# Unread products out where their operand was there already, modulation factors spread at waits, output projections by tile, LayerNorm statistics by halves

## The reference

```python
def first_block(x, p, positions, w_in, w_o, ...):
    for i in range(DEPTH):
        h = x @ w_in[i]
        q, k, v, qi, ki, wi, u, vs = jnp.split(h, split_points, axis=-1)
        ...
        a_out = dsa_attention(q, k, v, qi, ki, wi)
        b_out = spatial_gating(jax.nn.gelu(u), jax.nn.gelu(vs), sgu_w[i], sgu_b[i], ...)
        mix = jnp.concatenate([a_out, b_out], axis=-1) @ w_o[i]
        x = layer_norm(ALPHA * x + mix, ln1_g[i], ln1_b[i])
        gate, up = jnp.split(x @ w_ffn_in[i], 2, axis=-1)
        ffn = (jax.nn.silu(gate) * up) @ w_ffn_out[i]
        ple = (p[i] @ w_ple[i]) * jax.nn.sigmoid(x @ w_ple_gate[i])
        x = layer_norm(ALPHA * x + ffn + ple, ln2_g[i], ln2_b[i])

def second_block(x, c, positions, ada_w, ada_b, ...):
    for layer in range(DEPTH):
        mod = cond @ ada_w[layer] + ada_b[layer]
        sh1, sc1, g1, sh2, sc2, g2 = jnp.split(mod, 6, axis=-1)
        h = modulate(rms_norm(x, norm_mix[layer]), sh1, sc1)
        y = even_mixer(h, ...) if layer % 2 == 0 else odd_mixer(h, ...)
        x = x + g1[:, None, :] * y
        h = modulate(rms_norm(x, norm_mlp[layer]), sh2, sc2)
        x = x + g2[:, None, :] * squared_relu_mlp(h, mlp_w1[layer], mlp_w2[layer])
```

## Time and profile before

| | |
|---|---|
| three runs | 1359.42, 1356.29, 1351.66 us; median 1356.29 |
| profiled execution | 1356.18 us; span 1354.4 us, mean granted clock 0.994 |
| PE, PEld | 1308.6 us (97%), 1072.3 us (79%) |
| DVE, ACT, POOL | 921.8 us (68%), 655.2 us (48%), 113.7 us (8%) |
| unread products (L1507) | 191, 51.8 us busy |

### The profile page before, as it was taken

One profiled execution on the slowest core, in us unless ns is written; L12 is line 12 of the kernel. 1 busy time (PEld: TensorE's weight loads), 2 busy tenths in 40 slices (PEclk: granted clock), 3 DMA queues, 4 the chain that ended last, 5 costly groups with the idle time before them and its releaser, 6 DMA issues.

```text
span 1354.4 us, 16107 instructions
## 1 busy us (share of the span) xinstructions
PE 1308.6 (97%) x6466; PEld 1072.3 (79%) x6466; DVE 921.8 (68%) x1237; ACT 655.2 (48%) x886; POOL 113.7 (8%) x146
## 2 busy tenths in 40 slices
PE   8999999998999999999998989999999998999998
PEld 6877888887877788888798867888887766888886
DVE  5967777766685777775779756866666985644444
ACT  6644444443563544444475444544446554654542
POOL 2001000000000100000234200000004500000000
PEclk9999999999999999999999999999999999999999
DMA  9615677873642578885263303876764421445450
GB/s 373 235 63 195 241 307 308 309 275 129 224 142 98 214 265 308 308 308 209 84 210 117 109 32 114 323 295 244 299 248 170 160 105 34 173 174 184 182 186 31
DMA packets 41114, 270.36 MB, mean 200 GB/s; under 512 B 4656, under 2 KB 4672, under 8 KB 12880
## 3 DMA queue, kind: packets, MB, share of 16 engines
q1 hardware_dynamic: 38288, 259.83, 52.1%
q0 software_dynamic: 2464, 8.98, 1.9%
q10 hardware_dynamic: 288, 0.52, 0.1%
HBM read 268.27 MB, written 1.05 MB: 199 GB/s over the span
## 4 chain that ended last, share of the span: by engine, by line
PE 84%; DVE 10%; ACT 3%; issue 2%; POOL 1%; DMA 0%; ACTq 0%; DVEq 0%; POOLq 0%
PE ps L1540 49%; PE ps L1530 25%; PE ps L1554 4%; DVE WB L1852 3%; PE ps L1639 2%; PE ps L1507 2%; PE ps L1615 1%; ACT E L1652 1%; DVE st L2062 1%; DVE st L2134 1%; ACT WB L1652 1%; ACT XTH L1652 1%; DMA GB<-xTd 0%; POOL st L1455 0%; DVE X L2151 0%
## 5 line engine op out<-in xcount | busy, mean ns | idle before, releaser
L1852 DVE TENSOR_TENSOR WB<-RAW,WB 128x2048 fp32r<-128x2048 f32 (+3 forms) x211 | 453.4, 2151 | 247.3 <-ACT WB L1652 246.9
L1652 ACT ACTIVATE WB<-RAW 128x2048 fp32r<-128x2048 f32 (+3 forms) x211 | 379.7, 1802 | 200.4 <-PE ps L1540 198.7
L1530 PE MATMUL ps<-WB,XTH 128*128 128x512 f32 (+3 forms) x1176 | 314.5, 389 | 11.0 <-ACT XTH L1652 8.7
L1540 PE MATMUL ps<-WB,XTH 128*128 128x512 f32 (+3 forms) x1176 | 305.3, 381 | 7.1 <-DVE WB L1852 7.0
L1540 PE MATMUL ps<-WB,XTL 128*128 128x512 f32 (+3 forms) x1176 | 303.7, 379 | 0.0
L1540 PEld LDWEIGHTS ps<-WB,XTH 128*128 128x128 f32 x1176 | 218.4, 189 | 48.1 <-DVE WB L1852 9.8
L1530 PEld LDWEIGHTS ps<-WB,XTH 128*128 128x128 f32 x1176 | 213.6, 190 | 49.7 <-ACT XTH L1652 11.4
L1540 PEld LDWEIGHTS ps<-WB,XTL 128*128 128x128 f32 x1176 | 218.9, 189 | 38.4
L1530 PE MATMUL ps<-WB,HTH 128*128 128x512 f32 (+1 forms) x452 | 127.0, 396 | 0.5 <-ACT HTH L1652 0.5
L1540 PE MATMUL ps<-WB,HTH 128*128 128x512 f32 (+1 forms) x452 | 126.5, 395 | 0.0
L1540 PE MATMUL ps<-WB,HTL 128*128 128x512 f32 (+1 forms) x452 | 126.4, 394 | 0.0
(11 more groups left out here) (177 smaller groups left out, 973.9 us busy)
## 6 DMA issues: line engine op xcount, KB each, us to landing
RAW<-W SPq DMA_DIRECT2D x220, 1024.0 KB, 4.9
RAW<-W SPq DMA_DIRECT2D x22, 768.0 KB, 4.3
VEC<-vecd POOLq DMA_DIRECT2D x10, 512.0 KB, 7.5
RAW<-W SPq DMA_DIRECT2D x8, 512.0 KB, 3.5
RAW<-W SPq DMA_DIRECT2D x4, 576.0 KB, 3.8
RAW<-W SPq DMA_DIRECT2D x2, 648.0 KB, 3.8
T<-sgwd POOLq DMA_DIRECT2D x2, 512.0 KB, 8.1
X<-xd SPq DMA_DIRECT2D x1, 1024.0 KB, 17.7
```

What stands on the lines that cost most here:

```text
L1530: eng.matmul(banks[b][:, 0:cw], x2[j][0], hi[:, j, c0:c0 + cw], start=first and j == 0, stop=False)
L1540: op = eng.matmul(banks[b][:, 0:cw], x2[j][0 if low_w else 1], (lo if low_w else hi)[:, j, c0:c0 + cw], start=False, stop=last and end and ...
L1652: return eng.activation(dst, src, f, **k)
L1852: eng.tensor_tensor(WB[:, it["raw"], 0:w], RAW[:, it["raw"], 0:w], WB[:, it["high"], 0:w].bitcast(F32), ALU.subtract).then_inc(*up("wl", n))
```

## The change

- Unread products: 191 before, 76 now. They are left out in front of turns of E, of projections and of transposes at 38 places and made fewer at four; the 11 at each of the three projections that open a stage of the second block become 2.
- Modulation factors: the transposes of `gain` leave the two input projections of the second block, where they were woven in as eight groups of four. Each factor is now made in one piece of eight transposes: one in the dilated attention, between the scores of its first two units, one ahead of each of the two MLPs' first projections and one ahead of the odd layer's input projection, the last three in the places of the unread products.
- `linear_k` goes by tile for w_o and the even output projection: all its items for tile 0, then all for tile 1; before, both tiles of an item came one after the other. The bank of a tile is taken when the tile starts.
- LayerNorm: the statistics of a half are taken right behind the addition that completes it. In the first block's layer 0, the low part of the next weights is issued ahead of the second LayerNorm's passes over tile 1.
- `hold`: in the odd layer's second attention the low parts are issued from the third step on.

```diff
-        def linear_k(name, lhs, evac, ready, turned=False):
+
+        def linear_k(name, lhs, evac, ready, turned=False, by_tile=True):
             its = chunk_items(name)
             assert len(its) <= cur["pairs"]
-            w, g, ps = its[0]["w"], uid(), [take(), take()]
+            w, g, ps = its[0]["w"], uid(), [None, None]
             advance()
             its = its[::-1] if turned else its
-            for it in its:
-                for t in range(2):
-                    yield from ready(it["a"], t)
-                    b, fr = ps[t]
-                    lows([it])
-                    do("mm", it, t, "x", [(b, 0, w, (g, t) if it is its[-1] else None)], it is its[0], it is its[-1],
-                       wanted(lhs[t], "x", it), fr if it is its[0] else [], 0, it is its[-1], t)
-                    if t:
-                        used(it)
-                        advance(1)
-                    if it is its[-1]:
-                        evac(t, b, ("mm", (g, t)))
-                    yield
+            for it, t in ([(it, t) for t in range(2) for it in its] if by_tile else
+                          [(it, t) for it in its for t in range(2)]):
+                yield from ready(it["a"], t)
+                if ps[t] is None:
+                    ps[t] = take()
+                b, fr = ps[t]
...
-        def attention(units, scale, filler=None, steps=1, pads=(), first=0, between=()):
+        def attention(units, scale, filler=None, steps=1, pads=(), first=0, between=(), hold=0):
...
-                    turns(units[k - 1], pads[k - 1] if k <= len(pads) else 2)
+                    turns(units[k - 1], pads[k - 1] if k <= len(pads) else 0)
...
-                if k < n - 2:
+                if hold <= k < n - 2:
                     lows(old)
...
+        ln_sts = [None, None]
+
+
+        def ln_half(key, t, c, after):
+            if c == 0:
+                ln_sts[t] = col(12)
+            do("ln_half", key, t, c, ln_sts[t], after)
+
+        def ln_tile(key, t, between=None, before=None, halfway=None):
+            mv = col(2)
+            do("ln_stats", key, ln_sts[t], mv)
...
-                fill = linear2("w_in", "x", xt_w, [put_sel, put_gelu(1)], mid_in, pad=(6, 0), mid_at=2)
+                fill = linear2("w_in", "x", xt_w, [put_sel, put_gelu(1)], mid_in, pad=(2, 0), mid_at=2)
...
-                              [("kd", (i, t, 2))] + t_pe, 6, t, pad=0 if t else 2)
+                              [("kd", (i, t, 2))] + t_pe, 6, t, pad=i if t == 0 else 0)
...
-                             [("kd", (i, t, 1))] + t_pe, 0, t, pad=0 if t else 2)
+                             [("kd", (i, t, 1))] + t_pe, 0, t)
...
+                    ln_half((i, 1, t), t, c, rw[t][-1])
                     if c and t:
-                        x_n[1] = ln_tile((i, 1, 1), 1, rw[1], halfway=lambda: advance(1))
+                        x_n[1] = ln_tile((i, 1, 1), 1, halfway=lambda: advance(1))
...
-            attention(units, 0.125, fill, first=3)
+            attention(units, 0.125, fill, first=1, pads=(0, 2, 2))
...
-            run(linear2("w_ple_gate", "x", xt_w, [put_g(0), put_g(1)], mid1, pad=(0, 3), mid_at=1))
+            run(linear2("w_ple_gate", "x", xt_w, [put_g(0), put_g(1)], mid1, mid_at=1))
...
+                ln_half((i, 2, t), t, c, ("add_out", (i, t, c)))
                 if c == 0:
                     return
 
                 def between():
                     if t and i == 0:
                         xt_w[0][:] = to_XT(X, 8, x_n[0], 0)
+                        advance(1)
 
                 before = norm_sums(0, x_n[0]) if t and i else None
-                x_n[t] = ln_tile((i, 2, t), t, [("add_out", (i, t, c)) for c in range(2)], between, before,
-                                 (lambda: go(0, pad=14)) if t and i else None)
-                if t:
+                x_n[t] = ln_tile((i, 2, t), t, between, before, (lambda: go(0, pad=14)) if t and i else None)
+                if t and i:
...
+        def gain(layer, k):
             assert len(mod_w[(layer, 3 * k + 2)]) == 4
-            if hf == 0:
-                vg_w[k] = []
-            g = uid()
-            b, fr = take()
-            do("gain", g, layer, k, hf, b, mod_w[(layer, 3 * k + 2)], fr, list(vg_free[k]))
-            vg_w[k].append(("gain", g))
-            give(b, ("gain", g))
+            vg_w[k] = []
+            for hf in range(2):
+                g = uid()
+                b, fr = take()
+                do("gain", g, layer, k, hf, b, mod_w[(layer, 3 * k + 2)], fr, list(vg_free[k]))
+                vg_w[k].append(("gain", g))
+                give(b, ("gain", g))
...
-                gs = [lambda k=k, hf=hf: gain(0, k, hf) for k in range(2) for hf in range(2)]
-                run(weave(dils(0, 1), [[gs[0], mch[1, 1][0], mch[0, 1][1]], [gs[1], mch[1, 1][1]],
-                                       [gs[2], ch[0, 0][0], ch[0, 1][0]], [gs[3]]]))
+                run(weave(dils(0, 1), [[mch[1, 1][0], mch[0, 1][1]], [mch[1, 1][1]],
+                                       [ch[0, 0][0], ch[0, 1][0]]]))
...
-                attention(units, 96 ** -0.5, fill, (4, 3, 2, 2, 2, 0, 0, 0))
+                attention(units, 96 ** -0.5, fill, (4, 3, 2, 2, 2, 0, 0, 0), pads=(0, 0, 0, 0, 0, 2))
...
-                                      base, t, pad=0 if t or base else 2)
+                                      base, t)
...
-                                                                  for c in range(2)], mid, pad=(11, 0), mid_at=1), part((3, 4))),
-                          [[ch[0, 0][0]], [gs[0], ch[0, 1][0], ch[0, 0][1]], [gs[1], ch[0, 1][1], ch[1, 0][0]],
-                           [gs[2], ch[1, 1][0], ch[1, 0][1]], [gs[3], ch[1, 1][1]], [ch[3, 0][0], ch[3, 1][0]]]))
+                                                                  for c in range(2)], mid, pad=(2, 0), mid_at=1), part((3, 4))),
+                          [[ch[0, 0][0]], [ch[0, 1][0], ch[0, 0][1]], [ch[0, 1][1], ch[1, 0][0]],
+                           [ch[1, 1][0], ch[1, 0][1]], [ch[1, 1][1]], [ch[3, 0][0], ch[3, 1][0]]]))
...
-                attention(units, 0.125, fill, (2, 1, 1, 0, 0, 0), pads=(2, 2, 3, 3), between=between)
+                attention(units, 0.125, fill, (2, 1, 1, 0, 0, 0), pads=(0, 0, 0, 3), between=between)
...
+                if i == 0:
+                    gain(0, 0)
+                    yield
                 while normed:
                     normed.pop(0)()
                     yield
                 for t in range(2):
                     xo_w[t].extend(to_XT(MIX, 4, [keys_[t]["out"]], t))
                 yield
-                yield from linear_k(nm_out, xo_w, gated_put(i, 0, 0, xg), ready)
+                yield from linear_k(nm_out, xo_w, gated_put(i, 0, 0, xg), ready, by_tile=i == 0)
...
-            attention(units, 0.125, fill, (1, 1, 2, 1, 1, 1, 1, 1) if i else 1, first=3 if i else 0)
+            attention(units, 0.125, fill, (1, 1, 2, 1, 1, 1, 1, 1) if i else 1, pads=(2, 2) if i else (2,), hold=2 if i else 0)
...
+                    gain(i, 1)
...
-            mid = (lambda go=go: go(1, pad=2))
+            mid = (lambda go=go: go(1))
...
-                    gen = linear2("mlp_w1_2", "x", xt_w, [put_f(0), put_f(1)], mid, pad=(11, 0), mid_at=1)
+                    gen = linear2("mlp_w1_2", "x", xt_w, [put_f(0), put_f(1)], mid, pad=(2, 0), mid_at=1)
...
+                    if t:
+                        gain(1, 0)
...
-            def ln_stats(key, t, sts, mv, after):
-                for e in after:
-                    on.wait_ge(*at(*e))
-                for j in range(2):
-                    op = eng.bn_stats(sts[:, 6 * j:6 * j + 6], X[:, t, j * 512:j * 512 + 512])
-                op.then_inc(*own.up())
-                on.wait_ge(*own.at())
+            def ln_half(key, t, c, sts, after):
+                on.wait_ge(*at(*after))
+                eng.bn_stats(sts[:, 6 * c:6 * c + 6], X[:, t, c * 512:c * 512 + 512]).then_inc(*up("ln_half", (key, c)))
+
+            def ln_stats(key, sts, mv):
+                for c in range(2):
+                    on.wait_ge(*at("ln_half", (key, c)))
                 eng.bn_aggr(mv, sts.rearrange("p (c k) -> p c k", k=6)).then_inc(*up("ln_mv", key))
```

More of the change, by code:

```diff
@@ L705, in program @@
         sel_free, pt_free, mix_free, t_pe = [], [], [[], []], []
-        def ln_tile(key, t, after, between=None, before=None, halfway=None):
-            sts, mv = col(12), col(2)
-            do("ln_stats", key, t, sts, mv, after)
+        ln_sts = [None, None]
[6 more added lines that the diff above has]
+            do("ln_stats", key, ln_sts[t], mv)
             if before:
@@ L1098, in program @@
                 run(dils(4))
-                ltw = [turn_halves([MIX[:, t, k * 128:k * 128 + 128] for k in range(5)], lnw[t] + t_pe, HTH, HTL, t, pad=1 if t else 2)
+                ltw = [turn_halves([MIX[:, t, k * 128:k * 128 + 128] for k in range(5)], lnw[t] + t_pe, HTH, HTL, t)
                        for t in range(2)]
```

14 lines of the change are left out of this document (10 added, 4 removed).

## The result

| | before | after |
|---|---|---|
| median of 7 runs | 1357.94 us | 1348.13 us |
| profiled execution, span | 1356.18, 1354.4 us | 1346.15, 1344.4 us |
| mean granted clock, profiled | 0.994 | 0.988 |
| unread products | 191 | 76 |

The ratio is 0.9934, with a 95% interval from 0.9915 to 0.9953: faster by 0.66%, some 9 us. The forecast was 1345.9 us, a gain of 10.3.

The account below looks back on a forecast made before the run. PE was taken as the bound, busy 1308.6 of 1354.4 us, though other engines' waits limit gains. Terms summed to -14.5 us, clock falls added 4.2, giving -10.3: from 1356.2 to 1345.9 us, range 1337 to 1355.

Parts of the forecast that it names:

- Plain runs: 15 products in six runs ahead of projections where nothing waits soon after; removing them gains 3.2 us.
- first block's attention: Two layers: removed products gain 1.7 us each, w_o by tile costs 1.6 each through a longer XTH wait; together -0.2 us.
- LayerNorm: First LayerNorm of each layer: statistics by halves shorten the chain PE waits on, 1.0 us per layer, 2.0 together.
- Layer 1's start: Earlier low part removes a 2.54 us PE wait, new 2.3 us wait at second chunk; -2.2 us, -0.8 if clock falls.
- MLA: MLA attention: five runs of products go, but DVE has almost no slack; gain 0.9 us including a run behind it.
- Dilated attention: By-tile order removes two bank waits, seven runs go, new waits of 1.2 and 2.6 us; gain 4.2 us at full clock.
- Modulation factors: Four transpose groups leaving the odd input projection gain 1.4 us; those leaving the even one bring nothing.
- Odd attention: Removed products mostly bring nothing, because DVE is full or PE waits for exponentials; gain 0.4 us.
- The clock: Six PE waits of 2 us or more, three followed by half-speed stretches at 1.4 us each; cost 4.2 us.
- B: Rival: waits on ACT or DVE eat the gains from the new order; 1354 us, within 0.5%; chance 0.25.
- A: Rival: PE decides everywhere, so all 24.7 us of the removed products come off, 1331.5 us; chance 0.07.
- C: Rival: clock falls in attention stages thinned of products, making the kernel slower, say 1363 us; chance 0.10.

Follow-up runs that it names:

- the projection by item: The changed kernel with the even output projection item by item, as before the change: 1351.91 us, 0.9971 of before.
- the products alone: The kernel before with only 88 unread products taken out, the three runs of eleven staying: 1357.04 us, 1.0008 of before.
- the odd factors woven: The changed kernel with the odd layer's two modulation factors back in its input projection and the earlier products back at those two places: 1349.33 us.
- the statistics whole: The changed kernel with both halves' LayerNorm statistics taken behind the last addition, as before: 1349.26 us, 0.9947 of before.

## Why the prediction was right, and where its sum was off

The direction, the range and nearly the size were right: 9 us gained, 10.3 forecast. But it is a difference of two larger numbers, and both were too small. The sum of 14.5 already counts two falls of before as gone, 1.4 us each: the dilated one by name, and that of layer 1's start in the -2.2 that would else be -0.8. So from full clock to full clock it forecast 11.7, and for the clock, three falls in and two out, a net cost of 1.4. Measured, the change is worth 16.7 us at full clock, and the clock takes back 8.7 (16.7 lost against 8.0); at the lower price it is 14.1 and 6.1. That two errors of 5 and 7 us (2 and 5 at the lower price) nearly cancel in the total is luck.

*Plain runs, -3.2; first block's attention, -0.2.* Read run by run from how far the passes on either side moved, the six plain runs gave 3.1. In layer 0 the attention came out at +0.1: the kernel after is 1.52 us ahead at the transposes ahead of it (60.05 against 61.57) and 1.46 at the MIX transposes that end it (95.28 against 96.74). The wait of 2.3 was 2.10, and undoing the order gave 1.4 for the +1.6 of the sum. In layer 1 the clock fell behind the same wait.

*LayerNorm, -2.0.* Undone, 1.4 us came back in layer 0, so the term, 1.0 a layer, was a little small there; layer 1 was not read.

*Layer 1's start, -2.2, or -0.8 with a fall.* The transposes of X moved by 1.8 us more than what lay ahead of them, the new wait was 2.11 (forecast 2.3); the clock fell there again, and the transposes at 351.22 of before stand 0.7 us better than those at 329.65. The second value held.

*MLA, -0.9.* The step that DVE has no slack was right, and what follows from it was missed. PE's lost products became one wait, 1.86 us at the last turn, because DVE's maximum stood behind a low part (the rows at 758.94 and 761.14); it was not among my six waits of 2 us or more, and the clock fell for longer than anywhere before. From 728.84 of before to 776.34 the kernel lost 1.4 us instead of gaining.

*Dilated attention, -4.2.* From 776.34 of before to 813.30 it gained 4.3, with waits of 1.18 and 2.78 where 1.2 and 2.6 were forecast. The reason given for it, the banks, is not shown: with the projection by item PE waits as long in this stage, 4.00 us against 3.96, and loses clock.

*Modulation factors, -1.4.* 1.75 by the run that wove them back, 1.9 against before; nothing from the even projection, as forecast: the stretch where they had stood, 702.46 to 728.84 before and 697.25 to 723.64 now, is 26.4 us in both kernels, with a fall of the clock in it now, at 708.

*Odd attention, -0.4.* Shift of 9.63 us at 1073.93 of before, 10.01 at 1169.89: 0.4, but with two falls of its own against one before.

*The clock, +4.2.* This is the term that was mis-sized, and the step that failed is the count: only waits of 2 us or more were taken to cost a stretch. For those it was right, six waits as named and three falls behind them. Five more stretches of 3.4 us came behind waits of 1.97, 1.86 and 1.66 us (708, 763 and 1098, the last two twice as long), which were put at nothing, although before had such a fall behind 1.96 us at 728.84. The runs of the products alone show where such waits come from: with the fillers out, the waits of a stage grow by what the fillers took. Whether 1.4 us for a stretch was too little stays open: each takes 1.7 us of clock, which is 1.7 us at the full price and 1.2 at 0.7.

Of the rivals, B was wrong for the order of the work and A for the products. C's mechanism is what the run with the products alone shows, though it was not strong enough to make the whole slower. There the Trainium skill's section "A second HAM failure mode: psum-queue depth-cycling" (TensorE: Matmul & The Clock Gate) was the better guide than the row at 829 us that I set against it: the runs agree with it, 18.6 us of clock lost against 8.0 when only fillers were taken out. And that row was no rule: in the trace of the products alone the same place, behind the same wait (2.17 us at 828.20, 2.19 at 830.66 before), does lose clock, 0.72 from 829 to 835.

What stays open is which wait costs clock. The same wait of 2.10 us was followed by half speed in layer 1 and not in layer 0, and one of 2.78 was followed by none. In other executions it fell otherwise: with the odd factors woven both w_o waits of 2.1 us were followed by half speed, with the statistics whole neither was.
